# Opening loads in one queue, two conv blocks side by side, and x tiles scaled on VectorE

## What is computed

```
h   = rmsnorm(x, g_pre_mix)                     # 1024 wide
p   = h @ w_in -> xv | B | C | u | gate_conv | gate_pool
A   = (B * causal_dwconv3(C * xv)) @ w_out_conv
Bp  = pool_scale * groupwise_linear(trailing_mean(u) - u)
x   = x + rmsnorm((sigmoid(gate_conv)*A + sigmoid(gate_pool)*Bp) @ w_o)
x   = x + rmsnorm(relu(rmsnorm(x) @ w_up)**2 @ w_down)
```

## Time and profile before

| | |
|---|---|
| median of 3 runs | 970.77 us (969.71 to 971.44) |
| the profiled execution | 972.59 us, span 971.5 us on the slowest core (core 3) |
| spans of the eight cores | 961.8 to 971.5 us |
| TensorE busy with products | 932.3 us, 96% of the span |
| VectorE, ScalarE, GpSimd busy | 644.5, 360.5, 202.4 us |
| TensorE's granted clock, mean | 0.980 on core 3, 0.985 the median of die 0 |
| bytes read from HBM | 160.53 MB |

### The profile page before, as it was taken

How to read it: one execution, slowest core, us unless ns; L and a number is a source line. 1 busy time by engine, 2 the same in 40 slices (tenths; PEclk the granted TensorE clock), 3 DMA queues, 4 the chain that set the end, 5 groups by cost and what they waited for, 6 DMA issues and landing times.

```text
span 971.5 us, 15639 instructions; the slowest of 8 cores (961.8 to 971.5 us)
## 1 busy us (share of the span) xinstructions
PE 932.3 (96%) x5078; PEld 453.1 (47%) x5078; DVE 644.5 (66%) x960; ACT 360.5 (37%) x723; POOL 202.4 (21%) x203
## 2 busy tenths in 40 slices
PE   6899999999899999999998699999999999999997
PEld 3654444444354555455543244444444455544443
DVE  2567766674466666678849877769468766666087
ACT  2333342222344444333346455530124554520213
POOL 6530000000121220000016224330013243240022
PEclk7999999999899999999999799999999999999999
DMA  9699964545356754421449877894277639087026
GB/s 176 151 251 207 161 143 65 77 68 91 81 130 141 156 84 88 73 48 34 157 87 211 179 151 111 141 196 87 62 174 178 130 60 159 1 127 134 1 82 265
DMA packets 50575, 119.48 MB, mean 123 GB/s; under 512 B 21952, under 2 KB 22208, under 8 KB 50240
## 3 DMA queue, kind: packets, MB, share of 16 engines
q0 software_dynamic: 17712, 65.54, 41.6%
q1 hardware_dynamic: 32496, 52.64, 18.1%
q10 hardware_dynamic: 288, 0.30, 0.1%
HBM read 160.53 MB, written 19.01 MB: 185 GB/s over the span
## 4 chain that ended last, share of the span: by engine, by line
PE 82%; DVE 7%; issue 5%; POOL 2%; DMA 2%; ACT 2%; DVEq 0%; ACTq 0%; POOLq 0%
PE PS L139 81%; DVE AR L159 3%; DVE AR L169 3%; ACT AR L156 1%; DMA AR<-w_o 1%; POOL AR L164 1%; DMA AR<-x_p 1%; POOL AR L159 1%; POOL AR L129 0%; PE PS L143 0%; DVEq L224 0%; DVE STAT L427 0%; DVE AR L164 0%; ACT L156 0%; DVE FAC L498 0%
## 5 line engine op out<-in xcount | busy, mean ns | idle before, releaser
L139 PE MATMUL PS<-AR 128*128 128x512 bf16 (+1 forms) x4920 | 916.6, 349 | 20.1 <-DVE AR L159 14.2
L139 PEld LDWEIGHTS PS<-AR 128*128 128x128 bf16 x4920 | 441.9, 99 | 489.7 <-issue 39.7
L156 ACT ACTIVATE AR<-PS 128x512 f32<-128x512 f32 (+3 forms) x266 | 158.1, 601 | 347.6 <-PE PS L139 292.3
L159 DVE TENSOR_TENSOR AR<-AR 128x1024 bf16<-128x1024 bf16 (+10 forms) x268 | 234.5, 895 | 67.3 <-PE PS L139 29.5
L159 DVE TENSOR_TENSOR AR<-PS,AR 128x512 f32<-128x512 f32 (+1 forms) x249 | 159.3, 649 | 145.0 <-PE PS L139 133.4
L159 POOL TENSOR_TENSOR AR<-AR 128x512 bf16<-128x512 f32 (+1 forms) x66 | 115.2, 1755 | 391.3 <-DVE AR L169 220.5
L156 ACT ACTIVATE AR<-AR 128x1024 bf16<-128x1024 f32 (+3 forms) x131 | 95.2, 738 | 78.3 <-DVE AR L159 54.0
L169 DVE SCALAR_TENSOR_TENSOR AR<-AR,CS 128x512 f32<-128x512 f32 (+1 forms) x80 | 58.4, 730 | 40.0 <-ACT AR L156 19.8
L156 ACT ACTIVATE AR<-PS,CS 128x512 f32<-128x512 f32 (+1 forms) x80 | 48.9, 621 | 76.4 <-PE PS L139 66.8
L169 DVE SCALAR_TENSOR_TENSOR AR<-AR 128x512 bf16<-128x512 f32 (+4 forms) x100 | 60.4, 630 | 3.9
L156 ACT ACTIVATE AR<-AR,CS 128x512 f32<-128x512 f32 (+1 forms) x40 | 26.3, 658 | 93.5 <-DVE AR L159 93.5
(11 more groups left out here) (36 smaller groups left out, 97.2 us busy)
## 6 DMA issues: line engine op xcount, KB each, us to landing
AR<-x_p SPq DMA_DIRECT2D x32, 512.0 KB, 7.9
AR<-w_dn POOLq DMA_DIRECT2D x32, 512.0 KB, 14.8
AR<-w_m POOLq DMA_DIRECT2D x16, 768.0 KB, 9.2
AR<-w_up POOLq DMA_DIRECT2D x16, 768.0 KB, 9.1
x_d<-AR SPq DMA_DIRECT2D x17, 512.0 KB, 3.9
AR<-x_d SPq DMA_DIRECT2D x17, 512.0 KB, 9.1
AR<-w_a POOLq DMA_DIRECT2D x24, 256.0 KB, 10.3
AR<-w_a POOLq DMA_DIRECT2D x8, 768.0 KB, 9.2
```

What stands on the lines that cost most here:

```text
L139: return self.add("pe", lambda e: e.matmul(out, lhsT, rhs, start=start, stop=stop, **kw), reads=[lhsT, rhs], writes=[out], signal=sig, nam ...
L156: return self.add("act", lambda e: e.activation(out, in_, func, **kw), reads=rd, writes=wr, name=name)
L159: return self.add(eng, lambda e: e.tensor_tensor(out, in0, in1, op), reads=[in0, in1], writes=[out], name=name)
```

## The change

The norm's scaling is on VectorE for every tile. x0 stays on SP; 22 further loads (x1 to x10 and the chunks of blocks 0 to 3) are issued by POOL in one list, with no wait on another load. `head` and `head2` become one step: six PSUM banks are held for blocks 0 and 1, whose products are made tile by tile and chunk by chunk, both chunks of a tile as they are listed; `sl(i, cs_)` takes 0 to 2 for block 0's chunks and 3 to 5 for block 1's. There are 16 warming products at the start and 8 more before the transpose of tile 1. In `head3` the transpose of tile 5 moves behind block 2's chain and tile 7's norm.

```diff
-        def load_x(i, deps=()):
-            xload[i] = P.dma("sp", XS[i % 11], xsrc(i), "x%d" % (i % 11), name="xload", deps=deps)
+        def load_x(i, q="sp"):
+            xload[i] = P.dma(q, XS[i % 11], xsrc(i), "x%d%s" % (i % 11, "" if q == "sp" else q), name="xload")
...
-        def x_norm(i, eng="dve"):
+        def x_norm(i):
...
-            P.ts(eng, XN[i % 3], x, ss, None, ALU.mult, name="xn")
+            P.ts("dve", XN[i % 3], x, ss, None, ALU.mult, name="xn")
...
-            warm(22)
+            warm(16)
+            bk = [[grab() for _ in range(3)] for _ in range(2)]
+
+            def sl(i, cs_):
+                for c in cs_:
+                    a_mm(c // 3, 0, bk[c // 3], (i * 128, i * 128 + 128), (c % 3,))
             x_norm(0)
+            x_tr(0)
+            x_norm(1)
+            sl(0, (0, 1))
+            warm(8)
+            x_tr(1)
+            x_norm(2)
+            sl(1, (0, 1))
+            sl(0, (2,))
+            sl(1, (2,))
+            sl(0, (3,))
+            sl(1, (3,))
+            x_tr(2)
+            x_norm(3)
+            sl(2, (0, 1, 2, 3))
             for i in range(3):
-                x_norm(i + 1, "pool")
-                flush(2 if i < 2 else 9)
-                x_tr(i)
-            bk = (bank(), bank(), bank())
-            a_mm(0, 0, bk, (0, 128), (0,))
-            a_mm(0, 0, bk, (128, 256), (0,))
-            a_mm(0, 0, bk, (256, 384), (0,))
-            a_mm(0, 0, bk, (0, 128), (1,))
+                sl(i, (4,))
             x_tr(3)
-            a_mm(0, 0, bk, (128, 256), (1,))
-            a_mm(0, 0, bk, (256, 384), (1,))
-            for s in range(4):
-                a_mm(0, 0, bk, (s * 128, s * 128 + 128), (2,) if s < 3 else (0, 1, 2))
-            a_ew(0, 0, bk)
-        step(a_keys(0, 0), head)
-
-        def head2():
-            bk = (bank(), bank(), bank())
-            a_mm(1, 0, bk)
-            x_norm(4, "pool")
-            a_ew(1, 0, bk)
-            x_norm(5, "pool")
-        step(a_keys(0, 1), head2)
+            sl(3, (0, 1, 2))
+            a_ew(0, 0, bk[0])
+            sl(3, (3, 4))
+            for i in range(4):
+                sl(i, (5,))
+            x_norm(4)
+            a_ew(1, 0, bk[1])
+            x_norm(5)
+            for t in bk:
+                for b in t:
+                    drop(b)
+        step(a_keys(0, 0) + a_keys(0, 1), head)
...
             a_mm(2, 0, bk)
             x_tr(4)
+            x_norm(6)
+            a_ew(2, 0, bk)
+            x_norm(7)
             x_tr(5)
-            x_norm(6, "pool")
-            a_ew(2, 0, bk)
-            x_norm(7, "pool")
...
+        def first(*what):
+            for w_ in what:
+                if isinstance(w_, int):
+                    load_x(w_, "pool")
+                else:
+                    issue(("a", 0) + w_)
+                    done.add(("a", 0) + w_)
+        load_x(0)
+        first((0, 0), 1, (0, 1), (0, 2), 2, (1, 0), 3, (1, 1), (1, 2), (2, 0), (2, 1), (2, 2), 4, 5, 6, 7,
+              (3, 0), (3, 1), (3, 2), 8, 9, 10)
```

More of the change, by code:

```diff
@@ L1359, in issue @@
             wl[key] = P.dma("pool", dst, src, "w%d_%d" % (c, n), name="wload", deps=deps)
[L1361 to L1371, removed]
+        done = set()
+        def first(*what):
[8 more added lines that the diff above has]
+              (3, 0), (3, 1), (3, 2), 8, 9, 10)
         for s, st in enumerate(steps):
             for _, key in W.at.get(s, ()):
-                if key in [("a", 0, 1, 2), ("a", 0, 2, 0), ("a", 0, 2, 1), ("a", 0, 2, 2)]:
-                    pending.append(key)
+                if key in done:
                     continue
[L1378 to L1386, removed]
+                issue(key)
                 if key == ("a", 0, 7, 2):
```

## The result

| | before | after |
|---|---|---|
| median of 4 runs on one chip, us | 971.11 (969.71 to 972.67) | 981.05 (979.87 to 981.31) |
| ratio to before | 1 | 1.0101 [1.0086, 1.0116] |
| slowest span of the profiled execution, us | 971.5 (core 3) | 980.1 (core 1) |

The changed kernel is slower by 9.9 us; 5.5 were forecast. The mechanism came as forecast, but one step taken at nothing cost over three microseconds.

A forecast was written before the change was run, and what follows sets the result against it. The opening was taken as the bound: TensorE waits, mainly for GpSimd's scaling, and DMA idles, with any shift carried to the end. Terms 3.5 + 1.2 + 0.8 = +5.5 us gave 976.3 us from the median; range 970.0 to 981.0.

The forecast's parts named there:

- one step taken at nothing: x4's landing before tile 4's scaling on VectorE: on time, costing nothing; with SP's loads in between, 2.2 us late.
- first part: Opening up to VectorE's first multiplication z of block 0: z at 30.9 us instead of 27.43, shift +3.5 us.
- second part: From z to the end of tile 7's products, set by VectorE's line: 27.8 us instead of 26.6, +1.2 us.
- clock: TensorE's slices of tiles 4 to 6 after idling: one of two slowed by the lower clock level, +0.8 us.
- end of the narrow products: Point where tile 7's narrow products end, near 54.0 us before; later kernel unchanged; forecast sign: 57 to 61 us.
- first rival: SP's x11 to x14 take turns with the listed loads, x4 late by 2.2 to 7 us: 980 us; chance 0.15.
- Links: In the opening, each transpose start to evacuation end, with hand-over, between two bodies of TensorE's products: 2.1 us.
- Loads are covered: In the opening, x3 lands by 19.2 or 24 us, block 1's last weight two loads later: no load holds products up.
- The rule weighed: Whether SP's loads queue behind GpSimd's, x4 on time (sum 5.5 us), or DMA engines alternate between queues (sum 7.7 us).
- Loads out of order: SP's x11 to x14 take turns with the listed loads, making x4 late, middle 4 us: 980 us; chance 0.15.
- Faster: Evacuations on VectorE run ahead and feed TensorE, z 1.8 us earlier, then 5.7 us gained: 963.3 us; chance 0.14.
- No difference: Opening at full clock with x0 undisturbed (+1.6), z to tile 7's products no longer than before: 972.4 us; chance 0.13.

The follow-up runs named there:

- e1: The changed kernel with SP's x11, and all that SP loads behind it, held until x10 has landed; ratio to before 1.0024, +2.3 us.
- e2: The changed kernel with tile 5's transpose put back before block 2's chain, SP's loads left free; ratio to before 1.0050, +4.9 us.
- e3: The changed kernel with SP's loads held until x10 has landed and tile 5's transpose back before block 2's chain; ratio to before 0.9988, -1.2 us.
- e4: The kernel before with VectorE scaling tiles 1 to 7 and nothing else changed; ratio to before 0.9962, -3.7 us.

## Why the prediction was right and where it failed

**The sum, and what was measured for it.** Forecast: first part +3.5, second +1.2, clock +0.8, together +5.5 at the end of the narrow products. Measured on the mean of the cores: +3.8 and +4.2, together +8.0. The direction, the point to measure from and the two stages were right. The rest, carried unchanged, was right: 912.4 and 912.4. The median of 981.05 stands at the upper end of the stated range (970.0 to 981.0), nearer to the 980 of the first rival than to the forecast's 976.3; the end of the narrow products, 62.0, lies beyond the 57 to 61 given as a sign. Between the slowest cores of the two profiled executions, with rests of 917.5 and 918.1, the spans differ by 8.6 us; that the medians differ by 9.9 (8.4 to 11.3 by the interval) comes from the profiled execution of before, which was 1.5 above its median.

**First part.** The size was right, but partly by luck: two misses of some 3 us each cancelled. Links were forecast at 2.1 us, and the three of core 1 took 2.09 each (14.52 to 16.61, 20.75 to 22.84, 25.96 to 28.05). The warming products took 1.89 at a granted clock of 1.00, not the 2.6 of a middle between levels. "Loads are covered" failed for two weights, a_01 and a_10: 1.73 and 1.30 us on core 1. An earlier start hid this: x0 landed there at 5.0 and not at 8.0. The sum was made against core 3 of before, where x0 landed at 7.4; on the eight cores of before it lands at 4.9 to 7.4, and in after at 4.8 to 6.0. A sum against one core took that core's late x0 for the rule.

**Second part.** VectorE's line sets it, as forecast, and the waits for GpSimd came back as waits for VectorE. On core 1 the line from z to the end of tile 5's evacuation (the first of the two at 50.58, so 51.8) took 22.2 us instead of 18.8. The term that failed is the one for x4: "Taken at nothing; with SP's 4.25 loads in between it lands at 35.6, 2.2 late." It landed at 35.8. With z, and so the end of the chain, 1.3 us earlier than forecast, 2.2 became 3.5 by the forecast's own terms, and 3.77 was measured. e1 takes this away (VectorE's wait there is 0 on all cores), and z to end falls to 28.3, where 27.8 was forecast from core 3. The rest of the excess on core 1 is the 1.30 us stop before 59.83, for which the sum has no term: from 51.94 to the end 10.1 us instead of 8.8. On the mean of the cores such stops are 0.6 us; they are gone in e2 and e3 and nearly gone in e1, so a part of those savings is theirs.

**The rule weighed.** The prediction took the row of x4 in before, 8.8 us from issue to landing, for a load that went behind what was queued. After shows the misreading: SP's loads landed 8.4 to 8.9 us after their issue with far more queued on GpSimd, while GpSimd's own took 26.8. A time that does not grow with the other queue is no place in line. The shares of 56 to 72 us were the better row: they showed both queues moving.
The Trainium skill, DMA: Bandwidth & Descriptors, section "Queues, rings and completion order", has each DMA engine take turns between the queues with work; the trace agrees in that both queues moved at once (71.4% and 31.5% of the engines' time from 12 to 34 us), with x11 at 16.9 us ahead of x4 at 35.8.
"By turns the sum is 7.7 us" was the line to take; 8.0 was measured. That it comes so close is in part luck, since x4 cost more than its 2.2, the clock on core 1 nothing, and the stop is in no term.

**The clock.** +0.8 was set for slices at the lower level. On core 1 tile 4's slice took 3.98 us instead of 2.84 (granted clock 0.75 in that stage), but the next transpose then waited 0.90 us for VectorE: it cost nothing. On core 7 tile 5's slice took 4.47 us with no wait behind it: 1.6 lost. The 0.8 lies between these two cores; over all cores it was not added up.

**The rivals.** "Loads out of order" came true in its mechanism, beside the forecast and not in its place: it is the second part's excess. "Faster" had one true half: VectorE's cheaper scaling does feed TensorE (e4). It failed where the prediction said: each transpose stands behind the products of the tile before. "No difference" needs x4 on time and no late transpose; e3 is that kernel.

## What to carry to other kernels

An order of need in one queue holds in that queue alone: where a change takes loads off a second queue, look at what moves up there, and hold it with a wait on the last load of the list. Sum the line of the engine that sets the end with each input's landing beside it, and price a late one instead of taking it at nothing because one row allows it. Change one half at a time: here the cheap edit was a gain by itself, and the two costly ones fitted each other while hiding it.

## What was not expected of the hardware

- On core 1 of after an SP load of 512 KB, with at most two others in SP's queue, landed 8.4 to 8.9 us after its issue, whether 11 or 28 of GpSimd's loads were outstanding; x0, issued at 1.06 us into empty queues, took 4.0. Where SP's own queue was deep, the time grew: on core 2 of e1 seven loads issued within 4 us took 8.5 to 25.1.
- TensorE stopped for 0.48 to 1.30 us in the middle of tile 7's narrow products, put down to "issue", on seven of eight cores of after; two in e1 (0.5 us), and none in the other kernels. On core 1 a packet of the instruction queue moves near 57.6 us, with GpSimd's queue at 99% of the engines' time; on all nine cores with a stop the products go on 2.3 to 2.6 us after such a packet starts. That the instructions came late is a guess from these lines; it was not tried.
